# Up-projection pairs on Trainium2: the four weight-block sums formed on GpSimd out of a buffer of the pair's own

## What is computed

```python
h = rms_norm(x, norm2_g)                 # 256 x 2048
u = h @ w_up                             # 2048 x 11008, gate and value
u = causal_conv3(u, conv_w) + conv_b
gate, val = split(u, 2)                  # 5504 columns each
return x + (silu(gate) * val) @ w_down
```

## Time and profile before

| | |
|---|---|
| median of 3 runs | 1034.42 us (1033.8 to 1034.7) |
| the profiled execution | 1034.74 us, of which its span 1033.0 us |
| TensorE busy | 1027.1 us (99%), granted clock 0.999 |
| VectorE busy | 858.1 us (83%) |
| ScalarE busy | 810.5 us (78%) |
| GpSimd busy | 33.9 us (3%) |
| read from HBM, written | 224.81 MB, 14.30 MB |
| loads of raw pieces in the up-projection, issue to landing | 3.0 to 5.6 us, median 3.9 us |

### The profile page before, as it was taken

The page is one execution under the profiler, slowest core; times in us unless marked ns, Lnnn a source line. Parts: engine busy times, 40 slices in busy tenths (PEclk is TensorE's granted clock), DMA queues, the critical chain, the costliest instruction groups (busy, mean ns, idle before and its releaser), DMA issues.

```text
span 1033.0 us, 16320 instructions
## 1 busy us (share of the span) xinstructions
PE 1027.1 (99%) x5254; PEld 926.6 (90%) x5254; DVE 858.1 (83%) x1456; ACT 810.5 (78%) x1415; POOL 33.9 (3%) x43
## 2 busy tenths in 40 slices
PE   9999999999999999999999999999999999999998
PEld 8999999999988888888888888888889988888887
DVE  7788888878766656698998988988968799989988
ACT  7776776888858885889888898898887789856753
POOL 0101020000001101000000000000000000000000
PEclk9999999999999999999999999999999999999999
DMA  9667777776789899566676676666756757666664
GB/s 360 232 197 216 226 255 215 223 258 221 256 261 289 245 279 272 188 211 211 201 241 203 194 227 208 200 220 209 225 189 200 232 180 238 203 197 215 204 205 162
DMA packets 85023, 231.55 MB, mean 224 GB/s; under 512 B 20696, under 2 KB 24928, under 8 KB 84704
## 3 DMA queue, kind: packets, MB, share of 16 engines
q1 hardware_dynamic: 82240, 221.96, 65.7%
q0 software_dynamic: 2432, 8.39, 4.0%
q10 hardware_dynamic: 288, 0.40, 0.1%
HBM read 224.81 MB, written 14.30 MB: 231 GB/s over the span
## 4 chain that ended last, share of the span: by engine, by line
PE 91%; DVE 6%; DMA 2%; ACT 1%; issue 0%; SPq 0%; DVEq 0%; ACTq 0%
PE ps L797 13%; PE ps L799 13%; PE ps L798 13%; PE ps L585 7%; PE ps L587 7%; PE ps L586 7%; PE ps L870 4%; PE ps L872 4%; PE ps L871 4%; PE ps L775 3%; PE ps L777 3%; PE ps L776 3%; DVE w_lo L1494 2%; PE ps L821 1%; PE ps L607 1%; PE ps L819 1%
## 5 line engine op out<-in xcount | busy, mean ns | idle before, releaser
L1494 DVE TENSOR_TENSOR w_lo<-raw,w_hi 128x1024 fp32r<-128x1024 f32 (+2 forms) x422 | 470.4, 1122 | 131.3 <-ACT w_hi L967 129.5
L967 ACT ACTIVATE w_hi<-raw 128x1024 fp32r<-128x1024 f32 (+2 forms) x422 | 404.7, 970 | 140.5 <-PE ps L799 47.7
L797 PE MATMUL ps<-w_hi,xs 128*128 128x512 f32 (+1 forms) x640 | 240.0, 375 | 0.5 <-DVE w_lo L1494 0.5
L798 PE MATMUL ps<-w_lo,xs 128*128 128x512 f32 (+1 forms) x640 | 239.2, 374 | 0.0
L799 PE MATMUL ps<-w_hi,xs 128*128 128x512 f32 (+1 forms) x640 | 239.2, 374 | 0.0
L585 PE MATMUL ps<-w_hi,xs 128*128 128x384 f32 (+1 forms) x496 | 164.9, 332 | 0.3 <-DVE w_lo L1494 0.3
L586 PE MATMUL ps<-w_lo,xs 128*128 128x384 f32 (+1 forms) x496 | 161.8, 326 | 0.0
L587 PE MATMUL ps<-w_hi,xs 128*128 128x384 f32 (+1 forms) x496 | 161.8, 326 | 0.0
L797 PEld LDWEIGHTS ps<-w_hi,xs 128*128 128x128 f32 x640 | 120.9, 189 | 18.6 <-DVE w_lo L1494 3.3
L799 PEld LDWEIGHTS ps<-w_hi,xs 128*128 128x128 f32 x640 | 121.0, 189 | 15.4
L798 PEld LDWEIGHTS ps<-w_lo,xs 128*128 128x128 f32 x640 | 121.0, 189 | 15.3
(11 more groups left out here) (262 smaller groups left out, 1303.6 us busy)
## 6 DMA issues: line engine op xcount, KB each, us to landing
raw<-in_wrest SPq DMA_DIRECT2D x270, 512.0 KB, 4.2
raw<-in_win SPq DMA_DIRECT2D x117, 384.0 KB, 3.8
t_scratch<-in_wrest POOLq DMA_DIRECT2D x16, 512.0 KB, 7.6
raw<-in_wrest SPq DMA_DIRECT2D x16, 384.0 KB, 3.3
raw<-t_scratch SPq DMA_DIRECT2D x8, 512.0 KB, 3.6
p_scratch<-pdT SPq DMA_DIRECT2D x14, 192.0 KB, 2.8
p_read<-p_scratch SPq DMA_DIRECT2D x56, 48.0 KB, 2.7
xtok<-in_xtok SPq DMA_DIRECT2D x4, 512.0 KB, 14.3
```

The costliest lines, as they stand in the source:

```text
L797: pe.matmul(o, xh, wh, start=(k == 0), stop=False, skip_group_check=True)
L798: pe.matmul(o, xh, wl, start=False, stop=False, skip_group_check=True)
L967: act.activation(slot(w_hi, s, w), slot(raw, s, w), ACT.Copy).then_inc(hi_ready, 1)
L1494: dve.tensor_tensor(slot(w_lo, s, w), slot(raw, s, w), f32(slot(w_hi, s, w)), ALU.subtract).then_inc(split_done, 1)
```

## The change

"two" and "more" are both formed by GpSimd in SBUF (`weight_sums`). Pieces 8 and 9 of a pair are loaded whole into a buffer of their own, `pair_raw`, 2048 columns, which lies where the ring `a_s` of the down-projection comes to lie later. SP issues both loads right behind that of piece 5, without a further wait where a batch has one pair. GpSimd waits for both and for DVE's split of part 4 (whose raw slot "two" takes), and forms "two" with one addition of 2 x 512 columns; once that is done and DVE has split part 5, it forms "more" with two additions of 512 columns. DVE's `other_sums`, the scratch tensor and GpSimd's sixteen DMAs are gone.

The raw ring counts raw pieces now, that is, "left" and "lower" take no slot of it: ACT and DVE take these two from `pair_raw`, and the slot of a later piece comes from its piece number. The rings of high and low parts count parts as before. Matmuls, splits and their order stay.

```diff
-    t_d = nc.dram_tensor("t_scratch", (UP_SUMS * P, PW), F32, kind="Internal").ap()
...
         a_all = sb("a_all", FT * S, stack=hidden)
+        with ExitStack() as pair:
+            pair_raw = sb("pair_raw", 4 * BLOCK, stack=pair)
...
+        def up_raw_at(nb, par, j):
+            parts = up_parts(nb)
+            k = KT + j - len(parts) if j >= len(parts) else parts[j][1] + (parts[j][0] == "more")
+            return UP0 + KT * nb + k if isinstance(nb, int) else UP0 + KT + (0 if par else KT) + k
+        def up_raw(nb, par, j):
+            if in_pair(nb, j):
+                return slot(pair_raw, int(up_parts(nb)[j][0] == "lower"))
+            return slot(raw, up_raw_at(nb, par, j) % RING)
+        def up_landed(nb, par, j, turn=None):
+            if in_pair(nb, j):
+                n = len(UP_SEVEN)
+                return pair_landed, nb * (32 * n) + 32 * (UP_SEVEN.index(up_parts(nb)[j][1]) + 1 - UP_BATCHES[0] * n)
...
             def up_pieces(nb, par):
-                    sp.wait_ge(split_done, up_first(nb) + (j - RING + 1 + (j >= RING and parts[j - RING][0] == "lower")))
-                    if kind == "two":
-                        q = (nb - UP_BATCHES[0]) * n + UP_SEVEN.index(k)
-                        sp.wait_ge(t_built, 32 * (q + 1))
-                        sp.dma_start(slot(raw, s), t_d[q * P:(q + 1) * P, :]).then_inc(raw_landed[s], 16)
-                        continue
+                    if kind == "piece":
+                        last = place[k - RING] if k >= RING else k - RING
+                        sp.wait_ge(split_done, up_first(nb) + last + 1)
+                        if k >= RING and parts[last][0] == "two":
+                            sp.wait_ge(*up_landed(nb, par, last + 1))
+                        load(j, up_landed(nb, par, j)[0])
+                    if j + 3 < UP_LONG and parts[j + 3][0] == "left":
+                        if parts[j + 3][1] != UP_SEVEN[0]:
...
+                        load(j + 3, pair_landed)
+                        load(j + 4, pair_landed)
...
-                    if with_sums(nb) and j + 5 < UP_LONG and up_parts(nb)[j + 5][0] == "more":
-                        other_sums(nb, par, j + 5, turn)
...
-                pool.dma_start(row, upper).then_inc(t_built, 16)
-                pool.wait_ge(t_built, 32 * q + 16)
-                pool.dma_start(row.rearrange("p (k c) -> p k c", k=2), both[:, :, BLOCK:PW], accum_op=ALU.add,
-                               max_dma_last_dim=4096).then_inc(t_built, 16)
+            def weight_sums(nb, par, j):
+                parts = up_parts(nb)
+                left, lower, two, more = [up_raw(nb, par, j + i) for i in range(4)]
+                outer = pair_raw[:].rearrange("p (i c) -> p i c", c=BLOCK)[:, 0:4:3, :]
+                two_made, more_made = up_landed(nb, par, j + 2), up_landed(nb, par, j + 3)
+                last = [i for i in range(j) if parts[i][0] not in ("left", "lower")][-RING:]
+                pool.wait_ge(*up_landed(nb, par, j))
+                pool.wait_ge(split_done, up_first(nb) + last[0] + 1)
+                pool.tensor_tensor(two.rearrange("p (i c) -> p i c", c=BLOCK), outer,
+                                   left[:, BLOCK:PW].unsqueeze(1).to_broadcast([P, 2, BLOCK]), ALU.add).then_inc(two_made[0], 16)
+                pool.wait_ge(*two_made)
+                pool.wait_ge(split_done, up_first(nb) + last[1] + 1)
+                pool.tensor_tensor(more[:, 0:BLOCK], two[:, 0:BLOCK], lower[:, BLOCK:PW], ALU.add).then_inc(more_made[0], 8)
+                pool.wait_ge(more_made[0], more_made[1] - 8)
+                pool.tensor_tensor(more[:, BLOCK:PW], more[:, 0:BLOCK], lower[:, 0:BLOCK], ALU.add).then_inc(more_made[0], 8)
```

More of the change, by code:

```diff
@@ L328, in up_at, with in_pair @@
             return UP0 + KT + (0 if par else UP_LONG) + j
-        def up_round(nb, par, j, turn):
-            g = up_at(nb, par, j) // RING + 1
-            return g if isinstance(nb, int) else turn * (UP_LONG // 2) + g
+        def up_raw_at(nb, par, j):
+            parts = up_parts(nb)
+            k = KT + j - len(parts) if j >= len(parts) else parts[j][1] + (parts[j][0] == "more")
+            return UP0 + KT * nb + k if isinstance(nb, int) else UP0 + KT + (0 if par else KT) + k
+        def in_pair(nb, j):
+            return j < len(up_parts(nb)) and up_parts(nb)[j][0] in ("left", "lower")
+        def up_raw(nb, par, j):
[6 more added lines that the diff above has]
+                return pair_landed, nb * (32 * n) + 32 * (UP_SEVEN.index(up_parts(nb)[j][1]) + 1 - UP_BATCHES[0] * n)
+            at = up_raw_at(nb, par, j)
+            round_ = at // RING + 1 - AHEAD // RING
+            return raw_landed[at % RING], (round_ if isinstance(nb, int) else turn * (2 * KT // RING) + round_) * 16
         def up_width(nb, j, ahead):
@@ L533, in up_pieces, with load @@
             def up_pieces(nb, par):
-                n = len(UP_SEVEN)
                 parts = up_parts(nb)
-                for j, (kind, k) in enumerate(parts):
-                    s = up_at(nb, par, j) % RING
-                    if kind == "more":
-                        continue
-                    sp.wait_ge(split_done, up_first(nb) + (j - RING + 1 + (j >= RING and parts[j - RING][0] == "lower")))
-                    if kind == "two":
-                        q = (nb - UP_BATCHES[0]) * n + UP_SEVEN.index(k)
-                        sp.wait_ge(t_built, 32 * (q + 1))
-                        sp.dma_start(slot(raw, s), t_d[q * P:(q + 1) * P, :]).then_inc(raw_landed[s], 16)
[L546 to L549, removed]
+                place = {k + (kind == "more"): j for j, (kind, k) in enumerate(parts) if kind in ("piece", "two", "more")}
+                def load(j, landed):
+                    kind, k = parts[j]
+                    row = (UP0 - IN_PIECES + nb * KT + k + (kind == "lower")) * P
+                    sp.dma_start(up_raw(nb, par, j), wrest_d[row:row + P, :]).then_inc(landed, 16)
+                for j, (kind, k) in enumerate(parts):
+                    if kind == "piece":
[6 more added lines that the diff above has]
+                        if parts[j + 3][1] != UP_SEVEN[0]:
+                            used = max(i for i in range(j) if parts[i][0] == "lower")
+                            sp.wait_ge(split_done, up_first(nb) + used + 1)
+                            sp.wait_ge(*up_landed(nb, par, used + 2))
+                        load(j + 3, pair_landed)
+                        load(j + 4, pair_landed)
             rest_pieces(OUT0 + 8, UP0 + KT, PW, 0)
@@ L961, in _, with up_split @@
         def _(act):
+            def up_split(nb, par, j, turn, ahead):
+                w = up_width(nb, j, ahead)
+                act.wait_ge(*up_landed(nb, par, j, turn))
+                act.wait_ge(piece_used, up_first(nb) + j - (RING - 1))
+                act.activation(slot(w_hi, up_at(nb, par, j) % RING, w), up_raw(nb, par, j)[:, 0:w], ACT.Copy).then_inc(hi_ready, 1)
             def split_hi(G, s, round_, w=PW, free=True):
@@ L1472, in down_split @@
                 d = s + 4
-                split_hi(DOWN0 + d, d % RING, (DOWN0 + d) // RING + 1, PW if seven(d) is None else BLOCK)
+                split_hi(DOWN0 + d, d % RING, (DOWN0 - UP_EXTRA + d) // RING + 1, PW if seven(d) is None else BLOCK)
                 act_hi(d, d % FT, d % RING)
@@ L1491, in _, with split_lo @@
         def _(dve):
-            def split_lo(G, s, w=PW):
+            def split_lo(G, s, w=PW, whole=None):
                 dve.wait_ge(hi_ready, G + 1)
-                dve.tensor_tensor(slot(w_lo, s, w), slot(raw, s, w), f32(slot(w_hi, s, w)),
-                                  ALU.subtract).then_inc(split_done, 1)
+                from_ = slot(raw, s, w) if whole is None else whole[:, 0:w]
+                dve.tensor_tensor(slot(w_lo, s, w), from_, f32(slot(w_hi, s, w)), ALU.subtract).then_inc(split_done, 1)
             def x_lo(kt):
@@ L2014, in h_sums_lo @@
                 dve.tensor_tensor(kept_lo[:, c], ut[:, c], f32(kept_hi[:, c]), ALU.subtract).then_inc(h_lo, 1)
[L2016 to L2025, removed]
             def up_sums(nb, par, step):
@@ L2082, in up_long_steps, with up_batch @@
                         gate_times_value(pb, t)
-            def up_batch(nb, par, post=True, spill=True, ahead=UW, last=False, turn=None):
+            def up_batch(nb, par, post=True, spill=True, ahead=UW, last=False):
                 for j, part_ in enumerate(up_parts(nb)):
@@ L2128, in _ @@
             with dve.Fori(1, 4) as i:
-                up_batch(i * 2 + 1, 1, turn=i)
-                up_batch(i * 2 + 2, 0, turn=i)
+                up_batch(i * 2 + 1, 1)
+                up_batch(i * 2 + 2, 0)
             up_batch(FULL - 1, 1, ahead=LW)
@@ L2303, in _ @@
                                ALU.mult).then_inc(fox_ready, 1)
[L2305 to L2310, removed]
-                pool.dma_start(row, upper).then_inc(t_built, 16)
-                pool.wait_ge(t_built, 32 * q + 16)
```

(7 more changed lines are left out.)

13 lines of the change are left out of this document (5 added, 8 removed).

## The result

The changed kernel takes 1040.88 us (median of 8 runs, 1037.84 to 1043.62), the kernel before on the same chip 1033.83 us (8 runs, 1032.87 to 1035.21). The ratio is 1.0065, with a 95% interval of 1.0048 to 1.0082: slower by 7.05 us, where the forecast was 1.6 us and its range reached to 1044.0. The profiled execution took 1040.98 us, with a span of 1039.2.

A forecast was written before the change was run, and what follows sets the result against it. TensorE, busy 99% of the span, was taken as the bound. Transposes 0.7 us late, less 0.45 absorbed, cost 0.27 us in six batches, 1.6 us; other terms 0: 1036.0 us, range 1033.4 to 1044.0.

The forecast's parts named there:

- the free parts: Removed DVE additions, GpSimd DMAs and DRAM sums, SP's new waits, a later piece 6: each costed at 0.
- the late piece 6: Load behind the pair's two, landing near 541.5 instead of 540.2; ACT has room behind it, cost 0.
- The mechanism: GpSimd's addition locks out DVE's two-SBUF-input split of part 5; transposes 0.7 us late, 0.27 us at TensorE, six times.
- batch 1 absorbs: In batch 1 ACT's gaps for TensorE swallow the delay: cost 0.
- The chain: DVE's transposes, ACT's moves, ACT's splits, split of part 13, TensorE; absorbs about 0.45 us, more stops TensorE.
- the landing of the pair: Pieces 8 and 9, issued behind piece 5 at 533.5, land at about 540.2; bounds 537.2 and 542.9.
- between: Loads land at 541, delay 1.5 us: 6 us lost, 1040.7 us; no chance of its own given.
- Batch 2: Loads there before part 4 is split; GpSimd ends just when the split of part 5 is due: cost 0.
- A: Evacuations locked out too, or GpSimd's sum longer: 10 to 12 us lost, 1045.5 us; chance 0.25.
- B: Loads land before 539.5 or after 541.7, so GpSimd and the split don't collide: 1034.4 us; chance 0.23.
- C: Faster: relief of DVE and DMA engines ends small TensorE stalls, 2.2 us, 1032.2 us; chance 0.07.
- The step that hid part 6: Additions for "more" hold part 6's split until about 546.8; it ends near 548.0, wanted at 548.8: 0.8 us spare.

The follow-up runs named there:

- largest dose: Kernel before plus, in batches 3 to 8, one GpSimd addition of 2048 columns into a spare buffer, begun after the third evacuation: 1049.21 us, ratio 1.0152.
- dose runs: Kernel before plus one GpSimd addition per batch, batches 3 to 8, into a spare buffer; 512, 1024 and 2048 columns: 1033.59, 1038.99 and 1049.21 us.

## Why the prediction was right, and where it was off

**What bounds the kernel, and the free parts: right.** DVE's additions, the DRAM sums and GpSimd's DMAs, SP's waits and the late piece 6 are worth nothing: the run in which GpSimd only writes holds them all and stands at 0.9996. The profiled execution of the kernel after has 1.8 us outside its span, where the kernel before had 1.7: nothing is gained there.

**The mechanism: right.** The split of part 5 is locked, evacuations and transposes are not, the price of GpSimd's operations was 2.35 and 1.27 us (measured 2.38 and 1.28), batch 1 absorbs. The chain absorbs 0.37 us, read as 0.45. For the additions the Trainium skill (GPSIMD Engine Reference, Elementwise — side-by-side cycle accounting) has 4497 ns for 2048 columns; half of it, 2.25 us, is an estimate for 1024, and 2.38 us were measured. The largest dose, 2048 columns with both inputs from the same repeated 256, took 3.60 us; here the measurement decides.

**The size: off, 7.05 us for 1.6.** The term that was mis-sized is the landing of the pair, and through it the delay of the split of part 5. The prediction spaced the pair's loads by 1.2 us each behind piece 5 and had them land 6.7 us after its issue, at 540.2 in batch 4. Measured, in batches 1 to 8 the second load of the pair landed 7.7 to 8.7 us after the issue of piece 5: 6.8 to 7.9 us after its own issue, which starts 0.85 us after piece 5's. In the batches 4, 5, 7 and 8 GpSimd then begins not 1.4 us before the split of part 5 but 0.1 to 0.6 us before it, and by the prediction's own rule (the lock lasts for what is left of GpSimd's operation) the delay is 1.65 to 2.17 us, not 0.7. Four of the six like batches paid that, and two paid nothing. Such a landing was within the bounds that the prediction gave for batch 4, 537.2 to 542.9 behind an issue at 533.5, and its cost stood there as the case "between": landing at 541, 6 us, 1040.7. Near a threshold with this slope, one middle value was a poor stand-in for landings that spread over more than a microsecond. That this case's 1040.7 lies so near the measured 1040.88 is in part luck: it counts 1 us in each of six batches, where four paid 1.4 us or more and batch 2 another 1.06.

**Batch 2: wrong.** It was costed at nothing, on the ground that the loads land before part 4 is split. There too the pair landed late: the addition began at 458.97, during the evacuations, and held the split due at 460.16 for 1.06 us.

**Rivals.** A's own time, 1045.5 us, wasn't reached, and its mechanism is refuted: the evacuations stayed at 1.40 us a pair. Its "between" is the late landing told above. B (no collision) happened, in two batches of eight. C didn't happen: the run in which GpSimd only writes has the same small stalls as the kernel before, 2.2 us in all against 2.3.

**What would show it.** The prediction looked for a split of part 5 that starts 0.5 to 1 us after the last evacuation. It starts at once and is long instead; the rows of before that it rested on the earlier trace rows already had that form, 2.35 us in place of 1.82. And the loss is not at part 13 alone: in batches 4, 5, 7 and 8 parts 6 and 11 take 0.3 us or more each. The step that hid part 6 with 0.8 us to spare was worked out for transposes 0.7 us late; with the split of part 5 1.8 us longer, that of part 6 starts at 592.10, ends at 593.3 and is what TensorE waits for at 593.36.

**What stays open.** Why the time to landing of the pair's loads varies between 5.1 and 7.9 us was not tried. That a GpSimd instruction which only writes leaves DVE's split alone rests on two batches of one run; no run places a longer one there on purpose.

## What to carry to other kernels

Before work that reads SBUF is given to an idle GpSimd, list which of DVE's instructions will stand beside it: those with two inputs in SBUF stand still for all that is left of GpSimd's instruction, those with one input from PSUM and one from SBUF, and transposes, don't. Let the start of such work hang on the end of an instruction that must not be locked, rather than on the landing of a load, and keep it in short pieces. Here one number in one wait was worth 7 us.

## What the runs showed of the hardware

A lock between GpSimd and DVE shows as busy time: a 1.21 us split was reported as up to 4.18 us busy, with no idle time and no releaser. A GpSimd memset that overlapped such a split left it at 1.21 us. A DVE instruction with one PSUM input, one SBUF input and a scalar per partition ran at 1.40 us a pair with and without GpSimd beside it. The pair's loads of 512 KB, issued right behind another load, landed 5.1 to 7.9 us after their issue, where the raw loads of before took 3.0 to 5.6. And the GpSimd additions of the dose runs, both inputs of which were the same 256 columns repeated, were faster: 1.89 us for 1024 columns against 2.38 us.
